# Transposing three tiles from a rounded-type copy that the weight queue makes

## The reference

```
h = rms_norm(x, norm_g);  q,k,v,o,i,f,z_a,c_q,c_kv,k_r,z_b,g_a,g_b = split(h @ w_in)
y_a = (sigmoid(o) * norm(mlstm(q,k,v,i,f)) * silu(z_a)) @ w_a
y_b = (attention(c_q, c_kv, k_r) * silu(z_b)) @ w_b
y   = sigmoid(g_a) * y_a + sigmoid(g_b) * y_b
x   = x + y @ w_out
u   = rms_norm(x, mix_g) @ w_in_2            # Fourier mix and dilated attention of u
x   = x + concat(fourier, attention) @ w_out_2
x   = rms_norm(x + relu(rms_norm(x, mlp_g) @ w_up)**2 @ w_down)
```

## Time and profile before

| | us |
|---|---|
| median of 3 runs | 2096.67 (2096.65 to 2096.89) |
| the profiled execution's own time | 2096.84 |
| its span, from the first to the last instruction | 2095.0 |
| PE busy | 2075.7 (99%) |
| PEld / DVE / ACT busy | 1743.7 / 1451.5 / 1120.5 |

### The profile page before, as it was taken

The page is one execution under the profiler, slowest core; times in us unless marked ns, Lnnn a source line. Parts: engine busy times, 40 slices in busy tenths (PEclk is TensorE's granted clock), DMA queues, the critical chain, the costliest instruction groups (busy, mean ns, idle before and its releaser), DMA issues.

```text
span 2095.0 us, 25049 instructions
## 1 busy us (share of the span) xinstructions
PE 2075.7 (99%) x10006; PEld 1743.7 (83%) x10006; DVE 1451.5 (69%) x1892; ACT 1120.5 (53%) x1465; POOL 69.3 (3%) x84
## 2 busy tenths in 40 slices
PE   8999999999999999999999999999999999999998
PEld 6888888888888888888888888888888888888886
DVE  6877888875555786556554455566896896797794
ACT  6555555555444675554454454354564565465463
POOL 0000000000000020000000000000010000000000
PEclk9999999999999999999999999999999999999999
DMA  8545455565465544355755542455477477577564
GB/s 334 182 180 206 176 206 216 185 249 176 176 229 201 183 149 161 141 222 200 297 183 185 192 163 101 161 201 183 180 237 231 165 235 239 180 216 250 189 209 135
DMA packets 61909, 413.88 MB, mean 198 GB/s; under 512 B 7009, under 2 KB 7393, under 8 KB 14433
## 3 DMA queue, kind: packets, MB, share of 16 engines
q1 hardware_dynamic: 53568, 382.70, 50.9%
q0 software_dynamic: 7648, 28.84, 4.9%
q10 hardware_dynamic: 576, 0.73, 0.1%
HBM read 394.69 MB, written 8.39 MB: 192 GB/s over the span
## 4 chain that ended last, share of the span: by engine, by line
PE 96%; DVE 1%; ACT 1%; issue 1%; DMA 0%; POOLq 0%; POOL 0%; DVEq 0%; ACTq 0%
PE proj L646 15%; PE proj L648 15%; PE proj L647 15%; PE proj L1102 11%; PE proj L1106 6%; PE proj L742 4%; PE proj L743 4%; PE proj L744 4%; PE tbank L743 2%; PE tbank L742 2%; PE tbank L744 2%; PE tbank L605 2%; PE bank_a L742 1%; PE bank_a L744 1%; PE bank_a L743 1%; PE bank_b L743 1%
## 5 line engine op out<-in xcount | busy, mean ns | idle before, releaser
L1800 DVE TENSOR_TENSOR w_lo<-raw,w_hi 128x1024 fp32r<-128x1024 f32 x628 | 741.3, 1194 | 504.7 <-ACT w_hi L1213 497.8
L1213 ACT ACTIVATE w_hi<-raw 128x1024 fp32r<-128x1024 f32 x628 | 643.0, 1035 | 702.7 <-PE proj L648 462.9
L646 PE MATMUL proj<-w_hi,a_both 128*128 128x512 f32 x1280 | 512.7, 401 | 8.8 <-DVE a_both L1887 8.8
L648 PE MATMUL proj<-w_hi,a_both 128*128 128x512 f32 x1280 | 500.4, 391 | 0.0
L647 PE MATMUL proj<-w_lo,a_both 128*128 128x512 f32 x1280 | 499.2, 390 | 0.0
L646 PEld LDWEIGHTS proj<-w_hi,a_both 128*128 128x128 f32 x1280 | 241.1, 188 | 55.8 <-DVE a_both L1887 8.8
L648 PEld LDWEIGHTS proj<-w_hi,a_both 128*128 128x128 f32 x1280 | 240.7, 188 | 51.8
L647 PEld LDWEIGHTS proj<-w_lo,a_both 128*128 128x128 f32 x1280 | 241.2, 188 | 47.8
L1102 PE MATMUL proj<-a_both,w_hi 128*128 128x512 f32 x672 | 160.6, 391 | 0.3 <-DVE a_both L1846 0.3
L1102 PEld LDWEIGHTS proj<-a_both,w_hi 128*128 128x128 f32 x672 | 123.6, 188 | 24.5 <-DVE a_both L1846 0.5
L1800 DVE TENSOR_TENSOR w_lo_deep<-raw,w_hi_deep 128x1024 fp32r<-128x1024 f32 x86 | 98.2, 1163 | 44.7 <-ACT w_hi_deep L1213 44.6
(11 more groups left out here) (523 smaller groups left out, 3072.0 us busy)
## 6 DMA issues: line engine op xcount, KB each, us to landing
raw<-stream SPq DMA_DIRECT2D x358, 1024.0 KB, 4.8
nat<-stg POOLq DMA_DIRECT2D x35, 256.0 KB, 9.7
nat<-x SPq DMA_DIRECT2D x2, 1024.0 KB, 17.0
z_store<-z POOLq DMA_DIRECT2D x1, 2048.0 KB, 8.2
ga_store<-z POOLq DMA_DIRECT2D x1, 2048.0 KB, 12.4
gb_store<-z POOLq DMA_DIRECT2D x4, 512.0 KB, 7.4
yb<-z_store POOLq DMA_DIRECT2D x4, 512.0 KB, 9.3
ga<-ga_store POOLq DMA_DIRECT2D x1, 2048.0 KB, 8.1
```

The source lines that it names most:

```text
L646: nc.tensor.matmul(banks[t][:, :], ah, wh, start=first, stop=False)
L648: last = nc.tensor.matmul(banks[t][:, :], al, wh, start=False, stop=end)
L1213: A(hi_places[s][:, 0:width], src, ACT.Copy).then_inc(w_rounded, 1)
L1800: V.tensor_tensor(lo_places[s][:, 0:width], src, hi_places[s][:, 0:width].bitcast(f32), SUB).then_inc(w_rest, 1)
```

## The change

- A new tile `nat_r` of the rounded type (16 KB in a partition, where nothing else lives during the turns).
- SP's loop issues twelve copies into it, one for each chunk of each turn: 512 KB from SBUF to SBUF, in every partition two rows of 2 KB. The copy of chunk c stands behind unit first + 4c + 9 of the stream, and SP waits before it for both of the chunk's counts of `gated` or `res_ready`.
- The eight groups of each of the three turns (24 groups, 96 transposes) read `nat_r` and an identity of the rounded type, and write the bank seen as that type. They wait for the chunk's copy (`copied_r`) where they waited for the count before. All other transposes stay float32.
- The identity is a tile of its own (`ident_r`), loaded by POOL's queue ahead of its memsets; ACT's load of it goes.

```diff
+        nat_r = place("nat_r", [P, TT, D], f32r, 160.25)
...
+        ident_r = place("ident_r", [P, P], f32r, at)
...
-        ident = cst[:, CONSTS["ident"]]
+        ident = ident_r[:, :].bitcast(f32)
...
             for u in range(RING, UNITS):
                 sp.wait_ge(w_rest, FIRST_PIECE[u - RING] + 2)
                 sp.dma_start(raw[:, u % RING, :], stream[u]).then_inc(raw_landed[u % RING], 16)
+                for first, done, count in ((UNITS_B, gated, GATED_IN), (UNITS_OUT, res_ready, 0), (UNITS_OUT_2, res_ready, 8)):
+                    c, last = divmod(u - 6 - first, 4)
+                    if 0 <= c < 4 and last == 3:
+                        cols = slice(c * CW, (c + 1) * CW)
+                        sp.wait_ge(done, count + 2 * (c + 1))
+                        sp.dma_start(nat_r[:, :, cols].bitcast(f32), nat[:, :, cols]).then_inc(copied_r[c], 16)
...
             pool.dma_start(pos_i[:, :], pos_in).then_inc(pos_ready, 16)
+            pool.dma_start(ident_r[:, :], ident_in).then_inc(ident_ready, 16)
...
+            def group_r(g, n):
+                pe.wait_ge(copied_r[g // 2], 16 * (n + 1))
+                pe.wait_ge(used[readers[-2]], readers[-2].at(-1 if readers[-1] is readers[-2] else 0))
+                readers.append(by_dve)
+                by_dve.add()
+                for b in range(4):
+                    src = nat_r[:, b % 2, (2 * g + b // 2) * P:(2 * g + b // 2 + 1) * P]
+                    last = nc.tensor.transpose(tbank[(tr.n - aside.n) % 2][:, b * P:(b + 1) * P].bitcast(f32r), src,
+                                               ident_r[:, :])
+                last.then_inc(t_done, 1)
+                tr.add()
...
-                    ready(g)
-                    group(from_nat(buf, g), by_dve)
+                    if buf is nat:
+                        group_r(g, ready)
+                    else:
+                        ready(g)
+                        group(from_nat(buf, g), by_dve)
...
-            act.dma_start(cst[:, CONSTS["ident"]], consts_in[:, CONSTS["ident"]]).then_inc(ident_ready, 16)
```

More of the change, by code:

```diff
@@ L34 @@
 UNITS_MLP = UNITS - N_SLABS * 32
+UNITS_B, UNITS_OUT, UNITS_OUT_2 = UNITS_MLP - 16 - 32 - 32, UNITS_MLP - 16 - 32 - 16, UNITS_MLP - 16
 UNITS_IN = 1 + 4 * 6
@@ L95, in _columns @@
     return at
-N_CONSTS = _columns(CONSTS, [("ident", 128), ("attn_mask", 384), ("ml_mask", 256)])
+N_CONSTS = _columns(CONSTS, [("attn_mask", 384), ("ml_mask", 256)])
 EARLY = {}
@@ L159, in loop, with build @@
         t.n, t.reg = first[t] + count * k, None
-def build(nc, stream, x_in, xt_in, consts_in, early_in, params_in, pos_in, dft_in, alibi_in, fg_in, wf_in, z_store, ga_store, gb_store,
+def build(nc, stream, x_in, xt_in, ident_in, consts_in, early_in, params_in, pos_in, dft_in, alibi_in, fg_in, wf_in, z_store, ga_store, gb_store,
           out):
@@ L260, in build @@
         at = 192.25
+        ident_r = place("ident_r", [P, P], f32r, at)
+        at += P * 4 / K
         cst = place("cst", [P, N_CONSTS], f32, at)
@@ L421, in build @@
         res_ready = sem("res_ready")
+        copied_r = [sem(f"copied_r{c}") for c in range(4)]
         alibi_in_s = sem("alibi_in_s")
@@ L468, in _ @@
         def _(sp):
-            ident_cols = CONSTS["ident"]
             def x_part(i):
@@ L493, in _ @@
                 if u == RING + 4:
-                    sp.dma_start(cst[:, ident_cols.stop:], consts_in[:, ident_cols.stop:]).then_inc(cst_ready, 16)
+                    sp.dma_start(cst[:, :], consts_in).then_inc(cst_ready, 16)
             sp.wait_ge(out_ready, 2)
@@ L726, in gates_slot @@
                         last = nc.tensor.transpose(bank_a[:, 16 + 8 * t:24 + 8 * t], mrow[:, 1, P + t * P:P + (t + 1) * P],
-                                                   cst[0:8, 0:8])
+                                                   ident[0:8, 0:8])
                     last.then_inc(m_col, 1)
@@ L959, in projection @@
                 project(a_hi, a_lo, slot=tail)
-            y_tail, y_head, y_before = turn(nat, lambda g: pe.wait_ge(gated, GATED_IN + 2 * (g // 2 + 1)))
+            y_tail, y_head, y_before = turn(nat, 0)
             projection(b_head, b_before, y_tail)
-            r_tail, r_head, r_before = turn(nat, lambda g: pe.wait_ge(res_ready, 2 * (g // 2 + 1)))
+            r_tail, r_head, r_before = turn(nat, 1)
             projection(y_head, y_before, r_tail)
@@ L1082, in mix_slot @@
                     fourier_map(FG - 1)
-            m_tail, m_head, m_before = turn(nat, lambda g: pe.wait_ge(res_ready, 8 + 2 * (g // 2 + 1)))
+            m_tail, m_head, m_before = turn(nat, 2)
             projection(mix_slot, mix_before, m_tail)
@@ L1958, in gates_slot @@
                     chain(V.tensor_scalar(m, mrow[:, 0, P:P + TOK], 0.0, None, MAX))
-                    V.tensor_tensor(pick[:, :], cst[:, 0:8], cst[:, 32:40], ADD).then_inc(dve_seq, 1)
+                    dve.wait_ge(ident_ready, 16)
+                    V.tensor_tensor(pick[:, :], ident[:, 0:8], ident[:, 32:40], ADD).then_inc(dve_seq, 1)
                     seq.add()
@@ L2671, in _consts @@
     n = np.arange(P)
-    r[:, CONSTS["ident"]] = np.eye(P)
     ahead = np.where(n[None, :] > n[:, None], -BIG, 0.0)
@@ L2707 @@
         "xt": np.ascontiguousarray(i["x"][0].reshape(TOK, KT, P).transpose(2, 1, 0)),
+        "ident": np.eye(P, dtype=np.float32),
         "consts": consts,
@@ L2721 @@
     out = nc.dram_tensor("out", (TOK, D), f32, kind="ExternalOutput").ap()
-    build(nc, *(ap[n] for n in ("stream", "x", "xt", "consts", "early", "params", "pos", "dft", "alibi", "fg", "wf")), *stores, out)
+    build(nc, *(ap[n] for n in ("stream", "x", "xt", "ident", "consts", "early", "params", "pos", "dft", "alibi", "fg", "wf")), *stores, out)
     r = run_bass_kernel_spmd(nc, [arrays], core_ids=[0])
```

## The result

The changed kernel takes 2111.12 us (median, 2110.78 to 2111.29), the kernel before took 2096.78 beside it (2096.65 to 2097.22): the ratio is 1.0067, 95% interval [1.0054, 1.0079], 14.3 us slower. The forecast was 2103.1 with a range to 2110, so the direction was right and the size too small by 8 us. Rival B is the one whose mechanism came: copies in 2 KB packets, a first stall of 12 us, a sum of 2108. The measured time lies between it and B together with C, 2113.

A forecast was written before the change was run, and what follows sets the result against it. TensorE's own instruction stream, busy 99%, was taken as the bound. 2096.84 - 4.1 (transposes) + 7.1 + 0.6 + 1.1 (stalls in turns 1, 2, 3) + 1.8 (clock) = 2103.3, median 2103.1; range 2095.5 to 2110.

The forecast's parts named there:

- Rival B: Turn 1's last copy goes in 2 KB packets and stalls TensorE 12 us, sum 2108; chance 0.22.
- C: The rounded type doesn't make the transposes faster (load 0.11 us): 2108, or 2113 with Rival B; chance 0.1.
- the packets of the copy in turn 1: Fourth chunk's copy, 8 packets of 4 KB an engine, alternating with software-queue packets, lands about 1014.1: stall 7.1 us.
- The first packet's delay: Turn 1's last copy waits 3.3 us from issue to first packet, as a weight unit did.
- Rival D: No stall that matters: DMA engines take the copy at once and TensorE's clock holds; 2097, chance 0.17.
- The transposes' term: 96 rounded transposes at 0.065 us in place of 0.108 save 0.043 each, 4.1 us.
- The clock: After turn 1's stall TensorE falls to 1.2 GHz: nine matmuls each some 0.2 us too long, 1.8 us.
- Turns 2 and 3: The fourth chunk's copies land behind the weight unit ahead of them: stalls of 0.6 and 1.1 us.
- Copies 0 to 2, SP's waits and the identity's DMA: Copies of the first three chunks, SP's waits for the count and ident on POOL's queue are hidden: zero cost.

The follow-up runs named there:

- copy_on_pool: The changed kernel with the first turn's last copy issued by POOL on the software queue, ahead of alibi: 2108.44 us, ratio 1.0053.
- packets_1k: The changed kernel with the first turn's last copy in two DMAs of 256 columns each, in 1 KB packets: 2114.95 us, ratio 1.0086.
- loads_apart: loads_after with POOL's load of x into yb also issued some 60 us earlier: 2099.88 us, ratio 1.0013.
- loads_after: The changed kernel with POOL's loads of alibi, dft and wf held until the first turn's last copy has landed: 2106.43 us, ratio 1.0044.
- copies_only: The changed kernel with all twelve copies and the moved identity, but every group transposed in float32 from nat: 2096.99 us, ratio 0.9998.
- y_heads_f32: The changed kernel with groups 6 and 7 of the first turn back to float32 transposes from nat, all copies still made: 2097.82 us, ratio 1.0001.
- warm_pe: The changed kernel with 44 unread matmuls of 512 columns ahead of the first turn's wait for the fourth chunk's copy: 2110.89 us, ratio 1.0064.
- late_heads: loads_apart with groups 6 and 7 one piece later in turns 1 and 2, float32 without a copy in turn 3: 2095.65 us, ratio 0.9993.

## Why the prediction was wrong

- **The step that failed: the packets of the copy in turn 1.** The prediction took 4 KB a packet from a row of the software queue for a transfer on the hardware queue, and kept 2 KB as rival B. The queue sent 256 packets of 2 KB. While they went, the software queue sent 66 packets of 8 KB, 128 of 16 KB and 56 of 6 KB: almost one for each. That makes a stall of 11.6 us where the term had 7.1; B's 12 was near. Of the 4.5 us, 3.7 are packets (8.4 us from first to last, counted 4.65) and 0.7 the time from the last packet to the landing, which the term left out. copy_on_pool shows the same bytes in 128 packets on the software queue, packets_1k the same bytes in 512 and 3.9 us more. No run sent 4 KB packets on the hardware queue.
- **The first packet's delay was read rightly.** 4.0 us after the issue against the 3.3 read from the weight unit. Rival D's immediate start is out. That an idle queue takes 3.1 us for the whole copy is shown by loads_apart.
- **The transposes' term was mis-sized:** 4.1 forecast, 1.7 by the timelines, 2.0 by the pair (96 x 0.021). The step was "the load is no longer than 0.06, so the pair is 0.065". The load did stay short (a median of 140 ns, 139 in float32). But in the third turn's eight each load from the third on starts 50 to 53 ns after the matmul before it, about when that one's 53 ns of columns have gone by, and the matmul 34 to 35 ns after the load: load and stream stand one behind the other, 0.087. In float32 the load starts 1 to 2 ns after the matmul before it and the next matmul 107 ns later. So by these starts the two types order load and stream differently, which the term did not foresee; why, no run here took apart. The rule of the Trainium skill that the prediction cites (page "TensorE: Matmul & The Clock Gate", section "LDWEIGHTS (loading the stationary operand)"), an estimate of 107 ns a load, is contradicted for rounded transposes too: two pairs fit into less than two such loads.
- **The clock fell, and cost 2.2 us where 1.8 were forecast.** Ten matmuls stand 0.43 us apart in the mean, one more than forecast, and a group of transposes takes 0.54 instead of 0.29. loads_after shows it also behind a wait of 6.8 us, nearly the forecast's length.
- **Turns 2 and 3** stalled 0.93 and 1.07 us; forecast 0.6 and 1.1. Their copies wait behind the weight unit as costed.
- **Copies 0 to 2, SP's waits and the identity's DMA** cost nothing, as forecast: copies_only is within 0.4 us of the kernel before.
- **The range** ended at 2110 since B stood with the full transposes' gain and 12.0. With the measured 1.7 in place of 4.1, B's own working gives 2108 + 2.4 = 2110.4 us. Two errors, each with a rival of its own, came together, and the range left out their joint case: 4.5 us of stall and 2.4 us of gain, with 0.4 of clock and 0.3 of turn 2, are 7.6 of the 8.0 us.

## What to carry to other kernels

Before a DMA is put between a result and its reader, ask what the other queues hold at that moment. Of this copy's 13.1 us (3.1 alone), 4.0 stood before its first packet and 8.4 were its sixteen packets an engine, each next to one of the other queue's. Packet size has to be read on the queue that will carry the transfer, and the last chunk, the one with no time behind it, should keep the direct path (y_heads_f32 wins back 13.3 of 14.3 us with two groups). And a spacing worked out from matmuls of another kind is not the price of a pair: here it gave 0.065 us and the pair took 0.087, so the pair has to be measured in the type that it will have.

## What the runs showed of the hardware that was not expected

- One copy of two rows of 2 KB on each partition went as 256 packets of 2 KB from SP's queue and as 128 of 4 KB from POOL's.
- From SP's issue to the first packet it is 4.0 us when POOL's load of x is already running, 1.3 when nothing of POOL's runs and SP's unit before is just ending (the first three copies, and loads_apart), and 2.5 to 2.8 when some 3 us of SP's own unit are still ahead (the eight copies of turns 2 and 3). The queue round holds only from the first packet on. In between the engines serve x's 8 KB packets alone (102 in 2 us, 99.2% busy). It goes the other way too: x, issued at 1001.99 while a weight unit was on its way, had its first packet at 1005.97. Why a queue that comes second is let in so late was not settled.
- A 2 KB packet from SBUF to SBUF took 0.084 us (0.087 in loads_apart), where a quarter of an 8 KB packet's 0.31 is 0.077: reading SBUF costs little more than the packets' size says, and far from the double that the prediction's range allowed.
- SP's instruction for such a copy takes 0.61 us against 0.33 for a weight unit.
- Two kernels that left 1.7 us of idle time there had executions more than 2 us apart (warm_pe 2108.96 to 2111.46, loads_apart 2098.88 to 2101.12), most of the longer ones with a mean clock of 0.998 in place of 0.999. Only one of each left a trace, and the 27 executions of the kernel before beside late_heads are spread over 2.0 us as well, so that the idle time is the cause is not shown.
